# Attention of a two-layer block: two groups in flight, one-pass head normalisation, keys copied by ScalarE

## The reference

```
h  = modulate(rms_norm(x), ...)                   # 4 tiles of 128 tokens: 2 latent, 2 context
z  = h @ w_in                                     # Fourier 256, q 512, k 128, v 128, window q 256, k 128, v 128
q, k = rms_norm per head of 64 (8 q heads, 2 k heads), with a gain; rotary on the latent tokens
o_g = softmax(q k^T) v                            # 8 heads, keys: context and latent
o_w = softmax([q k^T banded, sink]) v             # 4 heads
f   = real part of a 2-D DFT of the Fourier columns
y   = (sum of three gated branches of f, o_g, o_w) @ w_out ;  x += gate * y
x  += gate2 * mixture of 16 experts               # its weights are 16 x 3 matrices of 1024 x 1024
```

## Time and profile before

| | |
|---|---|
| median of three runs | 2688.45 us |
| the profiled execution | 2693.58 us, span 2691.8 us, mean TensorE clock 0.896 |
| PE busy | 2237.4 us, 83% |
| DVE busy | 798.4 us, 30% |
| ACT busy | 354.7 us, 13% |
| chain that ended last | PE 66%, DMA 13%, DVE 13%, ACT 4% |

### The profile page before, as it was taken

The page is one execution under the profiler, slowest core; times in us unless marked ns, Lnnn a source line. Parts: engine busy times, 40 slices in busy tenths (PEclk is TensorE's granted clock), DMA queues, the critical chain, the costliest instruction groups (busy, mean ns, idle before and its releaser), DMA issues.

```text
span 2691.8 us, 21070 instructions
## 1 busy us (share of the span) xinstructions
PE 2237.4 (83%) x8356; PEld 1052.7 (39%) x8356; DVE 798.4 (30%) x1865; ACT 354.7 (13%) x800; POOL 0.2 (0%) x4
## 2 busy tenths in 40 slices
PE   3978889998788889887778978888888696777997
PEld 1433444444432333234334433222222344436873
DVE  3264520123311212223640231111111558733001
ACT  1014420011100000001151101000000132310000
POOL 0000000000000000000000000000000000000000
PEclk8978889999699999898798979998999798878999
DMA  8106851231089999992152517999999320122341
GB/s 318 63 32 250 313 181 46 86 125 63 0 373 429 429 429 428 424 419 95 64 210 79 211 63 326 428 430 428 429 429 424 119 94 19 45 70 102 125 149 70
DMA packets 106235, 593.16 MB, mean 220 GB/s; under 512 B 7999, under 2 KB 11791, under 8 KB 81435
## 3 DMA queue, kind: packets, MB, share of 16 engines
q1 hardware_dynamic: 101883, 583.43, 53.8%
q10 hardware_dynamic: 4256, 8.41, 0.9%
HBM read 590.77 MB, written 1.05 MB: 220 GB/s over the span
## 4 chain that ended last, share of the span: by engine, by line
PE 66%; DMA 13%; DVE 13%; ACT 4%; issue 3%; ACTq 1%; DVEq 0%
PE bank L1332 20%; PE bank L1555 17%; DMA weight_ring<-in_w_up_e 11%; PE bank L611 6%; PE bank L389 3%; PE bank L1288 3%; PE bank L629 3%; PE bank L1582 3%; PE bank L1455 3%; PE bank L1304 2%; PE bank L1526 2%; PE bank L1543 2%; PE bank L1483 1%; ACT arena L2196 1%; DMA arena<-in_w_up_e 1%
## 5 line engine op out<-in xcount | busy, mean ns | idle before, releaser
L1332 PE MATMUL bank<-weight_ring,arena 128*128 128x512 f32 (+1 forms) x1408 | 598.5, 588 | 7.5 <-DVE small L1780 2.7
L1555 PE MATMUL bank<-weight_ring,arena 128*64 128x512 f32 (+1 forms) x1664 | 502.5, 651 | 115.6 <-DMA weight_ring<-in_w_up_e 89.3
L1332 PEld LDWEIGHTS bank<-weight_ring,arena 128*128 128x128 f32 x1408 | 269.5, 192 | 333.1 <-issue 323.1
L1555 PEld LDWEIGHTS bank<-weight_ring,arena 128*64 128x64 f32 (+1 forms) x1664 | 145.8, 134 | 381.3 <-issue 376.9
L1288 PE MATMUL bank<-const,arena 128*128 128x128 f32 (+3 forms) x818 | 129.2, 314 | 122.0 <-DVE arena L1725 62.2
L1555 PE MATMUL bank<-arena 128*64 128x512 f32 (+1 forms) x384 | 183.7, 635 | 19.3 <-DMA weight_ring<-in_w_up_e 14.6
L1288 PEld LDWEIGHTS bank<-const,arena 128*128 128x128 f32 (+3 forms) x818 | 111.5, 182 | 171.5 <-DVE arena L1725 66.3
L1582 PE MATMUL bank<-weight_ring,arena 128*64 128x512 f32 (+1 forms) x800 | 177.7, 593 | 0.0
L611 PE MATMUL bank<-arena,weight_ring 128*128 128x256 f32 x704 | 154.5, 383 | 1.0 <-DVE small L1780 1.0
L2299 ACT ACTIVATE arena<-bank 64x512 f32<-64x512 f32 (+1 forms) x64 | 37.6, 588 | 824.6 <-PE bank L1555 824.5
L611 PEld LDWEIGHTS bank<-arena,weight_ring 128*128 128x128 f32 x704 | 135.5, 193 | 20.0 <-DVE small L1780 1.4
(11 more groups left out here) (326 smaller groups left out, 1659.0 us busy)
## 6 DMA issues: line engine op xcount, KB each, us to landing
weight_ring<-in_w_gate_e SPq DMA_DIRECT2D x52, 2048.0 KB, 15.3
weight_ring<-in_w_up_e SPq DMA_DIRECT2D x52, 2048.0 KB, 12.3
weight_ring<-in_w_down_e SPq DMA_DIRECT2D x50, 2048.0 KB, 12.3
weight_ring<-in_w_ada SPq DMA_DIRECT2D x24, 2048.0 KB, 12.3
weight_ring<-in_w_in SPq DMA_DIRECT2D x23, 2048.0 KB, 8.2
arena<-in_w_down_e SPq DMA_DIRECT2D x14, 2048.0 KB, 14.7
weight_ring<-in_w_mod SPq DMA_DIRECT2D x12, 2048.0 KB, 8.5
arena<-in_w_gate_e SPq DMA_DIRECT2D x12, 2048.0 KB, 15.9
```

The costliest lines, as they stand in the source:

```text
L1332: mm = pe.matmul(b[:, 0:c1 - c0], lhs[:, k, t * P:t * P + P], slot_view(r)[:, k, c0:c1], start=(k == 0), stop=(k == ks - 1))
L1555: mm = pe.matmul(banks_[n][c:c + R, :], xgT[:, KH * half + k, e, 0:R], wide(r)[:, k, n * 512:n * 512 + 512], start=(half == 0 and k == 0), ...
```

## The change

Four things are done at once. The head sums of all tiles are collected in one array, with one scale, one reciprocal and one square root for all of them. PE's Fourier products wait for the first part of `Z` alone, and DVE takes the first pair of them before it turns the window heads. The keys go through A banks and are copied by ACT. In attention, two groups are scored ahead, and on each engine the scores, exponentials or maxima of group i+2 stand behind the work on the probabilities of group i; PE's and DVE's `mod_step` stand behind those.

```diff
-        row_max, row_sum, sink_e, row_inv = (small[:, 48 + 4 * i:52 + 4 * i] for i in range(4))
+        row_max, row_inv = small[:, 48:52], small[:, 60:64]
+        row_sum = (small[:, 16:20], small[:, 20:24])
+        sink_e = (small[:, 24:28], small[:, 28:32])
...
@@ PE, mixer
-                pe.wait_ge(S("z_ready_dve"), due("z_ready_dve"))
-                pe.wait_ge(S("z_ready_act"), due("z_ready_act"))
+                pe.wait_ge(S("fourier_in_dve"), due("fourier_in_dve"))
+                pe.wait_ge(S("fourier_in_act"), due("fourier_in_act"))
...
+                pe.wait_ge(S("z_ready_act"), due("z_ready_act"))
                 pe.wait_ge(S("rope_ready"), due("rope_ready"))
@@ PE, turn_k: the same with freeA, bank_of("A", ...) and fullA in place of D
@@ PE, attention
                 scores(*groups[0])
+                scores(*groups[1])
                 for step, (s, t, grp) in enumerate(groups):
-                    if step + 1 < len(groups):
-                        scores(*groups[step + 1])
-                    if step < len(LATE_STEPS[l]):
-                        mod_step(*LATE_STEPS[l][step])
                     probs = probs_buf[step % 2]
                     keys = range(2 * s, TILES)
                     pe.wait_ge(S("probs_ready"), due("probs_ready", 4))
...
                             if h == 3:
                                 mm.then_inc(S("fullA"), 1)
+                    if step + 2 < len(groups):
+                        scores(*groups[step + 2])
+                    if step < len(LATE_STEPS[l]):
+                        mod_step(*LATE_STEPS[l][step])
                     pe.wait_ge(S("probsT_ready"), due("probsT_ready", len(keys)))
@@ DVE, head normalisation
+            def heads_norm(l, own):
+                spans = [(t, 0 if t in own else 8) for t in range(TILES)]
+                for t, h0 in spans:
+                    n = 10 - h0
+                    z = Z[:, t, GQ + h0 * HD:GQ + 10 * HD]
+                    sq = head_sq[:, 0:n * HD]
+                    dve.tensor_tensor(sq, z, z, ALU.mult).then_inc(S("dve_step"), 1)
...
+                    dve.tensor_reduce(head_ss[:, 10 * t + h0:10 * t + 10], sq.rearrange("p (h d) -> p h d", d=HD),
+                                      AX, ALU.add).then_inc(S("dve_step"), 1)
...
+                dve.tensor_scalar(head_inv, head_ss, 1.0 / HD, EPS, ALU.mult, ALU.add).then_inc(S("dve_step"), 1)
+                dve.reciprocal(head_inv, head_inv).then_inc(S("inv_ready"), 1)
                 dve.wait_ge(S("rstd_ready"), due("rstd_ready"))
+                for t, h0 in spans:
+                    for which, h, n in ((0, 0, 8), (1, 8, 2)):
...                      # two multiplications each, as before
@@ DVE, attention
                 take_scores(0, *groups[0])
+                take_scores(1, *groups[1])
                 for step, (s, t, grp) in enumerate(groups):
-                    if step + 1 < len(groups):
-                        take_scores(step + 1, *groups[step + 1])
...
                     for h in range(4):
                         dve.tensor_scalar(probs[:, h, 0:nk], probs[:, h, 0:nk], row_inv[:, h:h + 1], None, ALU.mult).then_inc(S("probs_ready"), 1)
                         dve.wait_ge(S("probs_ready"), due("probs_ready"))
+                    if step + 2 < len(groups):
+                        take_scores(step + 2, *groups[step + 2])
                     if step < len(LATE_STEPS[l]):
                         mod_step(*LATE_STEPS[l][step])
@@ DVE, mixer
+                take_z(0)
+                dve.memset(flag, 0.0).then_inc(S("fourier_in_dve"), 1)
+                take_z(1)
+                dve.wait_ge(S("z1_ready_act"), due("z1_ready_act"))
+                heads_norm(l, own)
+                for t in range(2):
+                    rope(t, GQ, 10)
+                take_z(2)
+                take_fourier()
+                dve.wait_ge(S("z_ready_act_v"), due("z_ready_act_v"))
+                for t in range(2):
+                    rope(t, WQ, 6)
+                dve.memset(flag, 0.0).then_inc(S("rope_ready"), 1)
+                for s in range(1, len(own) // 2):
                     dve.wait_ge(S("fT_done"), due("fT_done", 2))
+                    take_fourier()
+                dve.wait_ge(S("fT_done"), due("fT_done", 2))
                 for t in own:
                     take_q(t)
-                for t in range(TILES):
-                    take_k(t)
@@ ACT, attention
+                exponentiate(0, *groups[0])
+                exponentiate(1, *groups[1])
                 for step, (s, t, grp) in enumerate(groups):
...                      # copies of the transposed probabilities of group step
+                    if step + 2 < len(groups):
+                        exponentiate(step + 2, *groups[step + 2])
                     act.wait_ge(S("fullA"), due("fullA"))
...                      # copy of the result of group step
@@ ACT, the keys, after the Fourier copies and before attention
+            def take_k(t):
+                act.wait_ge(S("fullA"), due("fullA"))
+                b = bank_of("A", T.n["fullA"])
+                for p0 in ((0,) if t < 2 else (0, 64)):
+                    for d, s in split_heads(b, 2, kT, 0, t * P, p0):
+                        act.activation(d, s, ACT.Copy).then_inc(S("act_step"), 1)
+                        act.wait_ge(S("act_step"), due("act_step"))
+                act.activation(flag_a, zero, ACT.Copy).then_inc(S("freeA"), 1)
+                act.activation(flag_a, zero, ACT.Copy).then_inc(S("kT_ready"), 1)
```

More of the change, by code:

```diff
@@ L275, in build, with split_heads @@
         N_VEC, N_SMALL = len(vec_loads), len(small_loads)
+        def split_heads(b, pairs, dst, h0, cols, p0):
+            for odd in range(2):
+                src = b[64 * odd:64 * odd + 64, 0:pairs * P].rearrange("p (h i) -> p h i", i=P)
+                yield dst[p0:p0 + HD, h0 + odd:h0 + 2 * pairs:2, cols:cols + P], src
         block = ctx.enter_context(nc.Block())
@@ L1795, in heads_norm @@
                 dve.wait_ge(S("inv_ready"), due("inv_ready"))
                 dve.wait_ge(S("rstd_ready"), due("rstd_ready"))
[L1797 to L1800, removed]
+                for t, h0 in spans:
+                    for which, h, n in ((0, 0, 8), (1, 8, 2)):
+                        if h < h0:
+                            continue
+                        z3 = Z[:, t, GQ + h * HD:GQ + (h + n) * HD].rearrange("p (h d) -> p h d", d=HD)
+                        rs = head_rstd[:, 10 * t + h:10 * t + h + n].unsqueeze(2).to_broadcast([P, n, HD])
+                        dve.tensor_tensor(z3, z3, rs, ALU.mult).then_inc(S("dve_step"), 1)
+                        dve.wait_ge(S("dve_step"), due("dve_step"))
+                        dve.tensor_tensor(z3, z3, qk_gain[:, l, which, :].unsqueeze(1).to_broadcast([P, n, HD]), ALU.mult).then_inc(S("dve_step"), 1)
+                        dve.wait_ge(S("dve_step"), due("dve_step"))
@@ L1876, in attention @@
                     if grp == 2:
-                        dve.tensor_tensor(row_sum, row_sum, sink_e, ALU.add).then_inc(S("dve_step"), 1)
+                        dve.tensor_tensor(row_sum[step % 2], row_sum[step % 2], sink_e[step % 2], ALU.add).then_inc(S("dve_step"), 1)
                         dve.wait_ge(S("dve_step"), due("dve_step"))
-                    dve.reciprocal(row_inv, row_sum).then_inc(S("dve_step"), 1)
+                    dve.reciprocal(row_inv, row_sum[step % 2]).then_inc(S("dve_step"), 1)
                     dve.wait_ge(S("dve_step"), due("dve_step"))
@@ L1904, in take_z, with take_fourier @@
                             dve.wait_ge(S("freeD"), due("freeD"))
-                take_z(0)
-                take_z(1)
-                dve.wait_ge(S("z1_ready_act"), due("z1_ready_act"))
-                for t in range(TILES):
[L1910 to L1923, removed]
+                def take_fourier():
                     for c in range(2):
@@ L2158, in norm, with heads_norm @@
                 act.wait_ge(S("rstd_ready"), due("rstd_ready"))
[L2160 removed]
+            def heads_norm():
                 act.wait_ge(S("inv_ready"), due("inv_ready"))
[L2162 removed]
+                act.activation(head_rstd, head_inv, ACT.Sqrt).then_inc(S("rstd_ready"), 1)
                 act.wait_ge(S("rstd_ready"), due("rstd_ready"))
@@ L2178, in attention, with exponentiate @@
                 groups = [(t // 2, t, grp) for t in range(2 * streams) for grp in range(3)]
-                for step, (s, t, grp) in enumerate(groups):
+                def exponentiate(step, s, t, grp):
                     probs, neg = probs_buf[step % 2], row_neg[step % 2]
                     nk = 512 - 256 * s
-                    keys = range(2 * s, TILES)
                     act.wait_ge(S("scores_ready"), due("scores_ready"))
@@ L2192, in attention @@
                     act.wait_ge(S("exp_ready"), due("exp_ready"))
+                exponentiate(0, *groups[0])
+                exponentiate(1, *groups[1])
```

(11 more changed lines are left out.)

52 lines of the change are left out of this document (15 added, 37 removed).

## The result

| | before | after |
|---|---|---|
| median of 20 runs each | 2688.46 us | 2696.21 us |
| ratio, 95% interval | | 1.0032 [1.0018, 1.0047] |
| the profiled execution | 2693.58 us, span 2691.8 | 2692.22 us, span 2690.4 |
| mean TensorE clock | 0.896 | 0.894 |

A forecast was written before the change was run, and what follows sets the result against it. Attention was taken as bound by PE plus a short hand-off each step. -18.5 us ahead of attention, +26.7 and +6.9 in attention of layers 0 and 1 make +15.1: 2703.5 us, 8-in-10 range 2666 to 2726.

The forecast's parts named there:

- Ahead of attention: Heads, Fourier products and keys before attention: 11.7 us gained in layer 0, 6.8 in layer 1, together -18.5 us.
- Carry-through: What is saved in a mixer reaches the end; the DMA-bound stretch of the experts' loads only moves.
- The exposed additions: In attention, DVE's four segment additions (2.9 us) delay the scalings PE waits for; wide step 14.6 us at equal clock.
- What a fall costs: ... so 5.8 wide: Attention steps: a clock fall costs 6.7 or 5.0 us, so 5.8 in a wide step; 3.3 narrow, 4.5 mixed.
- I take a fall in 7 of 10 wide steps: Attention after the change: the clock falls in 7 of 10 wide steps and in every narrow one.
- the first step starts low anyway: First step of attention in each layer: low clock from the start, so a full 5.8 us is charged.
- the forecast's 41.5: Attention of layer 0: 41.5 us for the low clock over all steps, so 208.5 us in place of 181.8.
- (1): Attention: the clock falls about as often as before, costing the same 23 and 6 us; 2671 us; chance 0.30.
- (2): Attention: every gap drops the clock, in half of the cases before the transposes; +40 us, 2728; chance 0.15.
- (3): Attention: the upper clock holds through nearly all steps; -35 us, 2654; chance 0.08.
- (4): Ahead of attention: keys on ACT come late or the front gains half; +24 us, 2712; chance 0.07.
- all three gaps above 2.7 us ahead of transposes: Kernel before: gaps of 2.76, 3.47 and 8.27 us, said to have brought the low clock; counted against fewer falls.

The follow-up runs named there:

- e1: Changed front (one-pass head normalisation, early Fourier products, keys copied by ACT) with the attention loop of before: ratio to before 0.9927.
- e3: Changed kernel with DVE's additions of segment i moved behind the scalings of group i+1: 2614.23 us, ratio to before 0.9738.
- e7: Changed kernel with a same-size copy to scratch ahead of each of DVE's segment additions in attention: ratio to before 1.0238.
- e8: Kernel before with a same-size copy to scratch ahead of each of DVE's segment additions in attention: ratio to before 1.0005.
- e2: Front of before with the changed attention loop (two groups in flight): ratio to before 1.0091.
- e4: Changed kernel with PE's values product made twice in wide and three times in narrow steps that have a segment: 2665.72 us, ratio to before 0.9910.

## Why the prediction was right in direction and too large in size

Forecast +15.1, measured +7.7. Attention accounts for 10.7 us of forecast that didn't come; the 3.3 us the other way lie in the front and in code that the change doesn't touch, where single profiles differ by more than that.

- **Ahead of attention: right.** Forecast -11.7 and -6.8, measured -11.8 and -7.5 us; 1.7 of the 7.5 are the clock at the start of the dense products, so the change gives 5.8 there. The first query copy starts at 158.71 (forecast 158.4), attention at 171.93 (172). A 640-wide product took 0.825 us (taken 0.83), a key copy on ACT 0.378 (taken 0.41, between 0.2 and 0.60). A reciprocal of 40 elements took 0.40 and not about 0.2, which moved nothing, since DVE ends ahead of PE there.
- **Carry-through: right.** e1's ratio gives -19.6 us (interval -12.6 to -26.8), its stretches -17.4 without the clock in the dense products.
- **The exposed additions: right.** PE's waits are where they were forecast, each ended by the scalings, 2.7 to 4.1 us (forecast 2.7 to 3.8). At equal clock the pieces of layer 0 were to make 167 us. Measured, 204.8 less what each instruction took above its upper-level time (39.9) is 164.9. Layer 1: 88.1 of a forecast 89.4. e3, e7 and e8 show the mechanism from three sides.
- **The step that failed is "What a fall costs: ... so 5.8 wide", with "I take a fall in 7 of 10 wide steps" and "the first step starts low anyway".** I took the price from steps of before in which the fall came ahead of values and scores and stayed through the segment. After the change the transposes follow the gap, and in most wide steps they paid nearly alone. PE after, three wide steps:

```profile
189.32 3.50 PE L1296 MATMUL bank<-const,arena 128*128 128x128 f32 x16 [3.40 <-DVE arena L1880]
192.75 3.70 PE L1464 MATMUL bank<-arena 64*128 64x512 f32 x8
196.38 3.61 PE L1312 MATMUL bank<-weight_ring,silu_c 128*2 128x512 f32 x32
...
205.31 2.91 PE L1296 MATMUL bank<-const,arena 128*128 128x128 f32 x16 [3.44 <-DVE arena L1880]
208.15 7.19 PE L1464 MATMUL bank<-arena 64*128 64x512 f32 x8
215.28 5.84 PE L1312 MATMUL bank<-weight_ring,silu_c 128*2 128x512 f32 x32
...
226.80 3.53 PE L1296 MATMUL bank<-const,arena 128*128 128x128 f32 x16 [3.80 <-DVE arena L1880]
```

  Of the eight wide steps that have a segment and wide scores, six paid 1.4 to 1.7 us (transposes 3.2 to 3.5 in place of 1.97, scores 3.70 to 4.06) and two paid 6.7. The first step is among the cheap ones. So the clock was low behind every gap, where 7 in 10 were taken, and such a step paid 2.9 us on average, where 5.8 was taken for a fall. That is 11.6 + 11.5 = 23.1 us where the forecast had 2 x 18 = 36. Against it, the four narrow steps paid 17.4 and not 13.2. Net -8.7 of the -10.7 us by which attention missed its forecast (22.9 in the profile, 24.5 by e2, against 33.6); layer 1, all wide, holds 7 of them, though before's 102.5 there is the shortest of four profiles of the old loop. Above, 39.9 is the sum of all such surcharges of layer 0, and the forecast's 41.5 was close to it only because wide and narrow steps erred in opposite ways.
- **Rivals.** (1) is out: the mean clock went to 0.75, not 0.80. Its 2671 is what the front alone gives (e1, 2670), by coincidence. (2) was right on the transposes (they cost 19 us over both layers, 12 forecast) and wrong that the whole step would stay low: the segments of layer 0 took 57.4 us against 43.3 at the upper level (12 x 3.61), hardly more than before (54.9). (3) is out. (4) is out by e1. One count in favour of rival 2 was read wrong: of "all three gaps above 2.7 us ahead of transposes" the 2.76 us one has transposes at the upper level behind it, and only the values, after another 1.64 us of waiting, ran low:

```profile
360.98 1.09 PE L1288 MATMUL bank<-const,arena 128*128 128x128 f32 x8 [2.76 <-DVE arena L1882]
363.71 1.98 PE L1483 MATMUL bank<-arena 128*64 128x128 f32 x16 [1.64 <-ACT small L2201]
```

- **What I didn't price.** The prediction said that the additions were exposed, and didn't ask what it costs to put them one place later. That was the largest number of this case: 79 us between the ratios of the kernel after and e3.

## What to carry to other kernels

When an engine that sets the pace waits for a helper, read the helper's stream from that hand-over backwards and ask of each instruction who waits for it: one with no waiter ahead of one with a waiter can be on the path, however small (four instructions of 0.7 us in each of 16 steps cost 79 us here, clock included). Judge a reordering by the longest chain between two hand-overs, not by the wait that it removes. Then price the idle time on TensorE twice, and the second time as a range: the same instructions behind the same gap paid 1.5 us in one step here and 6.7 in another.

## What was not expected of the hardware

- **More work, less time.** e4's PE executes 1128 matmuls in attention of layer 0 where the kernel after has 872, and the stretch is 24 us shorter (181.0 against 204.8) at a mean granted clock of 0.88 against 0.75.
- **The same gap before the same instructions has two prices.** In the kernel after, gaps of 3.40 and 3.44 us stand before the same transposes, scores and segment. Behind the first, transposes that ran at the lower clock ended as it came back, with 64-row scores at full speed right behind (3.50, then 3.70); behind the second everything up to the segment paid (2.91, 7.19, 5.84). In the six cheap wide steps the granted clock was low when the transposes began or fell at most 0.5 us into them, and came back 2.8 to 3.9 us after that start. In the two dear ones it fell 0.85 us into them and came back only in the segment. But in e7 transposes that were low from their start (191.35, 3.68 us) had low scores behind them as well (7.19). So neither the length of the gap nor the instructions behind it set the price alone, and what does stays open.
- **Being busy did not always bring the clock back.** In every run the first scores of a layer, over 64 rows, held PE busy for 13.99 us without a gap and stayed at the lower clock to the end (0.87 us a record, where 3.70 us for eight make 0.46), before the change and after it. The 128x128 transposes of the cheap steps had it back within 3.9 us. What about the two kinds of matmul makes the difference (rows used, operands), or whether it is the kind at all, no run tells.
